# One gather and one block of transposes for the sample's rows of two experts, kept in the place of the affinities

## What is computed

```python
def expert_choice_moe(x, w_router, w_gate, w_up, w_down):
    xt = x.reshape(n_tok, D)
    aff = jax.nn.softmax(jnp.matmul(xt, w_router).astype(jnp.float32), axis=-1)
    gate, idx = lax.top_k(aff.T, cap)          # cap: 128 for the prompt, 64 for the sample
    xg = xt[idx]
    h = jax.nn.silu(jnp.einsum('ecd,edf->ecf', xg, w_gate)) * jnp.einsum('ecd,edf->ecf', xg, w_up)
    y = jnp.einsum('ecf,efd->ecd', h, w_down) * gate[..., None].astype(x.dtype)
    out = jnp.zeros_like(xt).at[idx.reshape(-1)].add(y.reshape(-1, D))
```

## Time and profile before

| | |
|---|---|
| median of three runs | 1789.37 us |
| the profiled execution | 1789.26 us, span 1787.5 us |
| TensorE matmul (PE) | busy 1744.2 us (98%), 10950 instructions |
| VectorE (DVE), ScalarE (ACT) | busy 1171.5 us (66%), 1060.7 us (59%) |
| GpSimd (POOL) | busy 404.3 us (23%) |
| TensorE's mean granted clock | 0.988 |

### The profile page before, as it was taken

The page is one execution under the profiler, slowest core; times in us unless marked ns, Lnnn a source line. Parts: engine busy times, 40 slices in busy tenths (PEclk is TensorE's granted clock), DMA queues, the critical chain, the costliest instruction groups (busy, mean ns, idle before and its releaser), DMA issues.

```text
span 1787.5 us, 31517 instructions
## 1 busy us (share of the span) xinstructions
PE 1744.2 (98%) x10950; PEld 1599.4 (89%) x10950; DVE 1171.5 (66%) x2300; ACT 1060.7 (59%) x2075; POOL 404.3 (23%) x560
## 2 busy tenths in 40 slices
PE   9999999899999999999999999999999999999994
PEld 9788898799999988888999999999999999999993
DVE  4442533477777862138777877777777777778776
ACT  4343333388888983333466766666666666666665
POOL 1322302244445542221110111101111011100112
PEclk9999999899999999999999999999999999999997
DMA  7556645654544743334786777868778687676785
GB/s 234 129 162 207 186 131 151 165 158 141 143 142 129 214 114 126 114 110 163 257 268 243 249 259 245 269 215 274 265 233 269 226 270 270 225 269 239 267 279 209
DMA packets 203636, 367.31 MB, mean 205 GB/s; under 512 B 39183, under 2 KB 64783, under 8 KB 202959
## 3 DMA queue, kind: packets, MB, share of 16 engines
q1 hardware_dynamic: 190268, 320.92, 53.6%
q0 software_dynamic: 13248, 44.96, 9.6%
HBM read 321.67 MB, written 50.45 MB: 208 GB/s over the span
## 4 chain that ended last, share of the span: by engine, by line
PE 47%; DVE 2%; DMA 2%; ACT 1%; POOL 1%; issue 0%; SPq 0%; DVEq 0%; ACTq 0%; POOLq 0%
PE psum L2152 21%; PE psum L2154 10%; PE psum L2171 3%; PE psum L2175 3%; PE psum L2173 3%; PE psum L2172 3%; PE psum L2174 3%; DMA own_rows<-x 1%; PE psum L2136 1%; PE psum L2133 1%; DVE raw_weights L1857 0%; DMA x<-y_s,index 0%; DMA rows_s<-xn,tokens 0%; DVE top_at L1447 0%; DVE affT L1449 0%
## 5 line engine op out<-in xcount | busy, mean ns | idle before, releaser
L2152 PE MATMUL psum<-x_parts,weight_parts 128*128 128x384 f32 x2048 | 583.5, 359 | 0.6 <-DVE x_parts L1844 0.6
L2154 PE MATMUL psum<-x_parts,weight_parts 128*128 128x192 f32 x2048 | 512.7, 250 | 0.0
L1795 DVE TENSOR_TENSOR weight_parts<-raw_weights,weight_parts 128x1024 fp32r<-128x1024 f32 x384 | 451.6, 1221 | 85.3 <-ACT weight_parts L1986 69.4
L1986 ACT ACTIVATE weight_parts<-raw_weights 128x1024 fp32r<-128x1024 f32 x384 | 382.2, 1055 | 30.7 <-PE psum L2175 16.2
L2154 PEld LDWEIGHTS psum<-x_parts,weight_parts 128*128 128x128 f32 x2048 | 391.1, 191 | 0.6
L2152 PEld LDWEIGHTS psum<-x_parts,weight_parts 128*128 128x128 f32 x2048 | 384.4, 188 | 1.4 <-DVE x_parts L1844 0.7
L603 PE MATMUL psum<-x_hi,w_parts 128*128 128x512 f32 x624 | 193.5, 390 | 0.0
L1735 POOL DMA_INDIRECT x<-y_p,index x15 | 24.1, 1609 | 625.1 <-DVE y_s L1852 376.8
L2013 ACT ACTIVATE h_parts<-up_sum 128x192 fp32r<-128x192 f32 x128 | 46.7, 365 | 169.8 <-DVE up_sum L1810 169.7
L848 POOL TENSOR_TENSOR logits_da<-logits_da 128x512 f32<-128x512 f32 (+1 forms) x96 | 103.9, 1104 | 165.4 <-DVE logits_da L936 165.4
L603 PEld LDWEIGHTS psum<-x_hi,w_parts 128*128 128x128 f32 x624 | 117.1, 188 | 26.8 <-issue 2.6
(11 more groups left out here) (220 smaller groups left out, 3181.4 us busy)
## 6 DMA issues: line engine op xcount, KB each, us to landing
raw_weights<-in_w_gate SPq DMA_DIRECT2D x32, 2048.0 KB, 7.8
raw_weights<-in_w_up SPq DMA_DIRECT2D x32, 2048.0 KB, 8.7
raw_weights<-in_w_down SPq DMA_DIRECT2D x32, 2048.0 KB, 9.5
mixed<-in_w_in SPq DMA_DIRECT2D x96, 256.0 KB, 4.2
q_parts<-q SPq DMA_DIRECT2D x188, 128.0 KB, 3.0
bias_da<-da_rows SPq DMA_DIRECT2D x31, 512.0 KB, 4.1
q<-mixed POOLq DMA_DIRECT2D x96, 128.0 KB, 3.1
mixed<-in_x SPq DMA_DIRECT2D x12, 512.0 KB, 6.8
```

The lines of the kernel that those rows point to most:

```text
L1795: dve.tensor_tensor(part_half(u, 1, half), src, part_half(u, 0, half).bitcast(F32), ALU.subtract).then_inc(split, 1)
L1986: act.activation(part_half(u, 0, half), src, ACT.Copy).then_inc(rounded, 1)
L2152: pe.matmul(out.rearrange("p (h n) -> p h n", h=2), w[:, 0, k, cols], x_parts[:, k, :, :], start=(k == 0), stop=False)
L2154: mm = pe.matmul(out[:, 0:SLOTS], w[:, 1, k, cols], x_parts[:, k, 0, :], start=False, stop=(k == KT - 1))
```

## The change

The 64 sample rows of the two experts of a pair are gathered together, 128 rows into `rows_s`, when the pair's first expert (i = 0) is fetched. They are transposed together by eight transposes with 128 rows, into banks 0 and 1, copied by one instruction of 1024 columns into `xT_sample`, a view of `affT`, and stay there for both experts. For a pair's second expert (i = 1) only the prompt's rows are gathered, transposed and copied; the last prompt piece then counts twice in `rows_transposed` and `xT_kept`. `xT` shrinks to the prompt's columns, so rounding and rest of the rows become two instructions each: the prompt's 128 and the expert's own 64 sample columns of each of the eight slices. For the joint gather VectorE copies the token numbers of the odd experts to the lower 64 partitions of the even experts' columns once, at the start; `tokens_ready` counts one more step.

```diff
-        rows_s = p.sb("rows_s", [CAP_S, D], F32R, stack=st)
+        rows_s = p.sb("rows_s", [2 * CAP_S, D], F32R, stack=st)
-        xT = p.sb("xT_e", [P, KT, SLOTS], stack=st)
+        xT = p.sb("xT_e", [P, KT, CAP_P], stack=st)
+        xT_sample = p.affT[:, :].rearrange("p (k i n) -> p k i n", k=KT, i=2)
...
                 def fetch_first():
-                    pool.wait_ge(tokens_ready, 1)
-                    for g, (rows, n, first) in enumerate(((rows_p, CAP_P, 0), (rows_s, CAP_S, SAMPLE_ROW))):
+                    for g, (rows, first) in enumerate(((rows_p, 0), (rows_s, SAMPLE_ROW))):
+                        pool.wait_ge(tokens_ready, g + 1)
...
                 def fetch(x):
...
-                    for g, (rows, n) in enumerate(((rows_p, CAP_P), (rows_s, CAP_S))):
+                    for g, rows in enumerate((rows_p, rows_s)[:2 - x.i]):
...
-                def keep_rows(e, order):
+                def keep_rows(x, order):
...
+                            dve.tensor_tensor(xT[:, ks, :], bank(p, 6 + c).rearrange("p (k n) -> p k n", n=P),
+                                              p.norm2[:, ks].unsqueeze(2).broadcast_to([P, 4, P]), ALU.mult
+                                              ).then_inc(xT_kept, 2 if x.i == 1 and c == 1 else 1)
                         else:
...
+                            dve.tensor_tensor(xT_sample.rearrange("p k i n -> p k (i n)"),
+                                              p.psum[:, 0:KT * P].rearrange("p (k n) -> p k n", n=P),
+                                              p.norm2[:, :].unsqueeze(2).broadcast_to([P, KT, P]), ALU.mult
+                                              ).then_inc(xT_kept, 1)
+                def split_rows(x, ks, step):
+                    for src, slots in ((xT[:, ks, :], PROMPT_SLOTS), (xT_sample[:, ks, x.i, :], SAMPLE_SLOTS)):
+                        last = dve.tensor_tensor(x_parts[:, ks, 1, slots], src, x_parts[:, ks, 0, slots].bitcast(F32),
+                                                 ALU.subtract)
+                    last.then_inc(x_split, step)
...
+                dve.wait_ge(tokens_ready, 1)
+                dve.tensor_copy(tokens[CAP_S:P, SAMPLE_ROW:SAMPLE_ROW + EXPERTS - 1],
+                                token_f[0:CAP_S, SAMPLE_ROW + 1:SAMPLE_ROW + EXPERTS]).then_inc(tokens_ready, 1)
...
-                            keep_rows(x.e + 1, PIECES)
+                            keep_rows(x.following(), PIECES[:3 - x.following().i])
...
+                def round_rows(x, ks, step):
+                    act.activation(x_parts[:, ks, 0, PROMPT_SLOTS], xT[:, ks, :], ACT.Copy)
+                    act.activation(x_parts[:, ks, 0, SAMPLE_SLOTS], xT_sample[:, ks, x.i, :], ACT.Copy
+                                   ).then_inc(x_rounded, step)
...
-                                k = 4 * c + b
-                                mm = pe.transpose(bank(p, 6 + c, P, b * P).bitcast(F32R), rows_p[:, k * P:(k + 1) * P],
-                                                  ident_r[:, :])
+                                out, k, rows = bank(p, 6 + c, P, b * P), 4 * c + b, rows_p
                             else:
-                                mm = pe.transpose(bank(p, 0, CAP_S, b * CAP_S).bitcast(F32R),
-                                                  rows_s[:, b * P:(b + 1) * P], ident_r[0:CAP_S, 0:CAP_S])
-                        mm.then_inc(rows_transposed, 1)
+                                out, k, rows = bank(p, b // 4, P, b % 4 * P), b, rows_s
+                            mm = pe.transpose(out.bitcast(F32R), rows[:, k * P:(k + 1) * P], ident_r[:, :])
+                        mm.then_inc(rows_transposed, 2 if x.i == 1 and c == 1 else 1)
...
-                        transpose_rows(x.e + 1, PIECES)
+                        transpose_rows(x.following(), PIECES[:3 - x.following().i])
...
-        p.affT = p.sb("affT", [LIST_ROWS, N_PROMPT])
+        p.affT = p.sb("affT", [P, N_PROMPT])
```

More of the change, by code:

```diff
@@ L1819, in hidden_rest @@
                     last.then_inc(h_split, 1)
-                def keep_rows(e, order):
+                def keep_rows(x, order):
                     for n, c in enumerate(order):
-                        dve.wait_ge(rows_transposed, 3 * e + n + 1)
+                        dve.wait_ge(rows_transposed, 3 * x.e + n + 1)
                         if n == 0:
-                            ge(dve, x_split, 2 * e)
+                            ge(dve, x_split, 2 * x.e)
                         if c < 2:
-                            ks, n, out = slice(4 * c, 4 * c + 4), P, slice(0, P)
-                        else:
[L1830 to L1834, removed]
@@ new lines, in split_rows, with rows_rest @@
+                def split_rows(x, ks, step):
[3 more added lines that the diff above has]
+                    last.then_inc(x_split, step)
+                def rows_rest(x):
+                    dve.wait_ge(x_rounded, 2 * x.e + 2)
+                    split_rows(x, slice(0, KT), 2)
@@ L1841, in first_rows_rest @@
                 def first_rows_rest(half):
-                    ks = slice(HALF_KT * half, HALF_KT * (half + 1))
                     dve.wait_ge(x_rounded, half + 1)
-                    dve.tensor_tensor(x_parts[:, ks, 1, :], xT[:, ks, :], x_parts[:, ks, 0, :].bitcast(F32),
-                                      ALU.subtract).then_inc(x_split, 1)
+                    split_rows(Expert(0, 0), slice(HALF_KT * half, HALF_KT * (half + 1)), 1)
                 def sum_sample_output(x, c):
@@ L1925, in _ @@
                     split_rest(Expert(0, 0), u, u)
-                keep_rows(0, FIRST_PIECES)
+                keep_rows(Expert(0, 0), FIRST_PIECES)
                 for half in range(2):
@@ L1949, in step @@
                         if z == 9 and not x.is_last:
-                            keep_rows(x.e + 1, PIECES)
+                            keep_rows(x.following(), PIECES[:3 - x.following().i])
                         if z == 11 and not x.is_last:
-                            rows_rest(x.e + 1)
+                            rows_rest(x.following())
                         if z == 14 and not x.is_last:
@@ L2051, in _ @@
                 for half in range(2):
-                    ks = slice(HALF_KT * half, HALF_KT * (half + 1))
                     act.wait_ge(xT_kept, half + 2)
-                    act.activation(x_parts[:, ks, 0, :], xT[:, ks, :], ACT.Copy).then_inc(x_rounded, 1)
+                    round_rows(Expert(0, 0), slice(HALF_KT * half, HALF_KT * (half + 1)), 1)
                 def step(x):
@@ L2077, in step @@
                             act.wait_ge(xT_kept, 3 * (x.e + 2))
-                            act.activation(x_parts[:, :, 0, :], xT[:, :, :], ACT.Copy).then_inc(x_rounded, 2)
+                            round_rows(x.following(), slice(0, KT), 2)
                         if z == 14:
@@ L2120, in _, with transpose_rows @@
                 mm.then_inc(lists_flipped, 1)
-                def transpose_rows(e, order):
-                    pe.wait_ge(gathered[0], 16 * (e + 1))
-                    ge(pe, xT_kept, 3 * e)
+                def transpose_rows(x, order):
+                    pe.wait_ge(gathered[0], 16 * (x.e + 1))
+                    ge(pe, xT_kept, 3 * x.e)
                     for c in order:
                         if c == 2:
-                            pe.wait_ge(gathered[1], 16 * (e + 1))
-                            ge(pe, up_summed, 8 * e - 1)
+                            pe.wait_ge(gathered[1], 16 * (x.r + 1))
+                            ge(pe, up_summed, 8 * x.e - 1)
                             pe.sem_inc(waits_taken_pe, 1)
@@ L2142, in _ @@
                 keep_busy(pe, p, 5, 22)
[L2143 removed]
+                transpose_rows(Expert(0, 0), FIRST_PIECES)
                 keep_busy(pe, p, 5, 7)
```

16 lines of the change are left out of this document (6 added, 10 removed).

## The result

The changed kernel takes 1779.79 us (median of 5 runs, 1778.45 to 1780.57) where the kernel before takes 1789.31 (5 runs, 1786.84 to 1790.17): ratio 0.9950, 95% interval 0.9939 to 0.9960. It is faster, as forecast; the median lies 0.6 us under the range of 1780.4 to 1785.2. Both were run again later: 1780.62 against 1789.14.

A forecast was written before the change was run, and what follows sets the result against it. TensorE's matmul queue was taken to bound the kernel, busy 1744.2 of 1787.5 us. From 1789.26, -8.7 in the expert loop and +1.3 at the start gave 1781.9 us; range 1780.4 to 1785.2.

The forecast's parts named there:

- Steady sum: Expert loop on TensorE: sample transposes removed or joined save 8.7 us over all changes of expert; bounds 6.2 and 9.2.
- Odd experts: Ahead of experts 1, 3 ... 15 the sample's transpose block goes: 0.90 us saved each, 7.2 in all.
- Even ones: Ahead of experts 2 ... 14, sixteen transposes all with 128 rows: 0.22 us saved each, 1.5 in all.
- The price of changing the rows: TensorE's weight loads around the 64-row sample block: 0.13 us lost going in and 0.11 coming out.
- Start: Start of the expert stage, up to the first product: 1.3 us longer, bounds 0.8 and 2.8.
- the gather: First sample gather, 128 rows instead of 64: 5.4 us from issue to landing against 4.91, +0.5; bounds 0 and +2.0.
- The index copy: Added VectorE copy at the start: hidden before GpSimd's first gather issue ends, pushing first weight splits by some 0.2 us.
- The terms behind the landing: Start of the stage: VectorE's copy +0.53, rounding +0.18, rest +0.16, change of rows after the sample block gone -0.1.
- What follows the last one moves as one piece.: Program's end: everything after the last sample transpose block shifts together, predicted difference 0.
- Rival A: Gaps at the transpose blocks come from waits in front, not the change of rows: 1784.4 us; chance 0.10.
- Rival B: TensorE's clock low when products start, from added idling: +1.6 us (1783.5) or +4.5 (1786.4); chance 0.13.
- Rival C: Copy, rounding and rest of the next rows become the path before the next expert's x_parts wait: 1820 us; chance 0.03.

The follow-up runs named there:

- the copy alone: Kernel before with only the change's copy of the sample's token numbers to the lower 64 partitions: 1787.90 us (0.9996).
- the splits held to the landing: Changed kernel with VectorE's splits of the first two weight units held until the prompt's first rows have landed: 1780.30 us, one run.
- one split ahead: Changed kernel with VectorE's split of the first weight unit ahead of its two copies (tokens and gates): 1780.61 us (0.9955).

## Why the prediction was right and where it failed

- **What bounds the kernel.** Right: TensorE's queue is the path, and matmuls taken out of it shortened the run by what they and their gaps took (8.33 us up to expert 14's last matmul, where 8.7 was forecast).
- **Steady sum, -8.7.** Right in mechanism, 0.4 too large. Odd experts: 0.88 (56.15 - 55.27) for seven of them and 0.74 for expert 1 (56.37 - 55.63), against 0.90. Even ones: 0.20 (56.15 - 55.95) against 0.22. Together 7 x 0.88 + 0.74 + 7 x 0.20 = 8.3. That the distance between the starts of weight loads is what a block costs was the author's reading, which no row of before shows; the steps bear it out, 0.88 measured for 0.90 read and 0.20 for 0.22. The price of changing the rows, 0.24 us read from the two gaps, was confirmed by the two runs with the block put back: 0.20 us a step (56.13 against 55.93).
- **Start, +1.3.** The step that failed is its first term, the gather, +0.5. It took the row of another gather of 128 rows for the new landing and GpSimd's issues for fixed. Measured: the way from issue to landing +1.1 (6.0 against 4.9), the first issue -1.03, together about 0.1. The index copy, priced at nothing because it is hidden, is what shortened the issue (1.10 us with the copy alone, where it was 2.13): it moved a VectorE split by 0.1 us. The terms behind the landing were right in their sum: from there to the first product 3.59 us before and 4.34 after, +0.75 against +0.53 + 0.18 + 0.16 - 0.1 = +0.77. One by one only VectorE's copy was (+0.54); the rounding cost 0.09 and the rest 0.07, and the -0.1 did not come, because VectorE's copy waits for the sample's block and not for what follows it. That the differences cancel is luck. And +0.88 is the first pair of profiles alone: in the second the kernel before lost as much to the clock in front of its first product, and the start cost nothing.
- **"What follows the last one moves as one piece."** It failed by 0.65: GpSimd's last drain, which ends the span, took 5.450 us with the old number of gathers and 4.797 with eight fewer. The prediction counted that GpSimd issues eight fewer and gave them no price.
- **Sum.** -8.3 + 0.9 - 0.65 = -8.1 for what belongs to the change, against the forecast -7.4: the gather and the drain forecast the time too high by 1.0, the steady sum too low by 0.4. The profiled pair shows -8.7: the cast came 0.73 later and `own_rows` landed 1.32 sooner, and both move by about as much between two profiles of the kernel before. The medians show -9.5 (-8.5 when both ran again); the 0.8 that the changed kernel's median lies under its profiled run stands in no profile, and its cause stays open. The forecast of -7.4 lies within the interval of the ratio (0.9939 to 0.9960 of 1789.31 is -10.9 to -7.2); the range was too narrow below, since it had no term for the end of the program, held the start to cost at least 0.8, and allowed 0.5 for noise where the last piece alone moved by 1.38.
- **Rival A**, waits: fell. The waits stayed in place in front of the repeated block of 128 rows, and there was no gap (its first load due at 903.47, there at 903.48).
- **Rival B**, the clock: its price was right, its cause was not. Where the products run through a whole stretch at a granted clock of 0.50 (866 to 869 us in the run with the splits held to the landing) it costs 1.6 us (57.19 - 55.63), against +1.6, worked out from the 0.50 at 854.60; where they meet the end of one, 0.76 (the kernel with the copy alone). But such a stretch also comes in the kernel before, from 854 to 858 in one profile (mean granted clock 0.57) and from 863 to 867 in the repeat (0.61); in the changed kernel from 855 to 859 (0.61), and from 864 to 868 in the repeat (0.57). In the changed kernel the first step took 55.63 and 55.72 us in the two profiles, 55.47 in the run with one split ahead, so the products lost at most 0.25 us to it. What brings the clock down no run shows.
- **Rival C**, the copies become the path: fell; no wait for `x_parts` from 870 us on.

## What to carry to other kernels

Read the cost of a small block on TensorE from the distance between weight loads (0.90 us read here, 0.88 measured), and look at its edges: going from 128 to 64 rows and columns and back lost 0.13 and 0.11 us here, so two blocks of half height are worth joining for their edges as well. When you cost a start-up at single events, let the issue times of a software queue be unknown too: here a hidden copy that moved a neighbour by 0.1 us changed an issue from 2.13 to 1.10 us. And compare a kernel with itself first: here the untouched ends moved by 1.4 us from one profile to the next.

## What the runs showed that was not expected

- Going from 128 to 64 array rows (and from 128 to 64 columns with them) costs 0.13 us and back 0.11, in both places where the block was put; transposes with 64 and with 128 rows keep nearly the same pitch (0.082 to 0.084 and 0.085 us).
- At the start of the stage GpSimd's issue of an indirect gather takes 0.97 or 1.10 us where no VectorE split runs as it begins, and 1.80 to 2.13 where one does.
- The last drain on GpSimd: 5.450 us, 4.797 with eight indirect gathers fewer, 0.08 us for each if they count alike, and the same 5.450 with 13248 packets and with 13504.
- TensorE's granted clock falls to 0.50 for 3.4 us at a time (from windows of 1 us) near the start of the expert stage in eleven of the twelve profiles, of either kernel; one (the first gather with 64 rows) shows none from 850 to 872 us. What it costs depends on what runs in it: nothing that shows in the first profiles of both kernels, 0.8 us where it meets the `keep_busy` matmuls in front of the first product, 1.6 where the product runs through it.
